# A hybrid encoder layer: the HGRN2 mixer in blocks of 704 tokens with seven block products

## The reference

```python
q, f, i, g = split(rmsnorm(x) @ w_in)               # 1024 -> 4 x 1024, 8 heads of 128
fg = lb + (1 - lb) * sigmoid(f); k = 1 - fg; G = cumsum(log(fg))     # in chunks of 64 tokens
scores = tril((q * exp(G - g_mid)) @ (k * exp(g_mid - G)).T)
o = scores @ i + (q * exp(G)) @ state
state = exp(g_last) * state + (k * exp(g_last - G)).T @ i
x = x + (rmsnorm(o) * silu(g)) @ w_out
x = x + (silu(h @ w_gate) * (h @ w_up)) @ w_down     # h = rmsnorm(x), 1024 -> 2816 -> 1024
```

## Time and profile before

| | |
|---|---|
| time, median of 3 runs | 2577.03 us (2571.08 to 2577.51) |
| the profiled execution | 2580.97 us, its span 2579.2 us |
| instructions | 42643, of them 14834 matmuls |
| TensorE busy | 2495.8 us, 97% of the span |
| VectorE, ScalarE, GpSimd busy | 70%, 53%, 22% |
| mean granted TensorE clock | 0.993 of full |
| DMA | 508.59 MB, 197 GB/s over the span |

### The profile page before, as it was taken

The page is one execution under the profiler, slowest core; times in us unless marked ns, Lnnn a source line. Parts: engine busy times, 40 slices in busy tenths (PEclk is TensorE's granted clock), DMA queues, the critical chain, the costliest instruction groups (busy, mean ns, idle before and its releaser), DMA issues.

```text
span 2579.2 us, 42643 instructions
## 1 busy us (share of the span) xinstructions
PE 2495.8 (97%) x14834; PEld 2341.2 (91%) x14834; DVE 1798.6 (70%) x2620; ACT 1355.0 (53%) x2370; POOL 576.0 (22%) x411
## 2 busy tenths in 40 slices
PE   7999999999999999998999999999999999999899
PEld 7999888887888778887999999999999999899899
DVE  6666556775776566767667767677666778878777
ACT  5555535655655555644455445555444545555454
POOL 6333233343554243420211012011101100000000
PEclk9999999999999999998999999999999999999999
DMA  7433565446556576535666656665657677877875
GB/s 266 157 117 116 161 202 174 141 139 229 176 188 202 160 243 192 195 105 169 204 203 194 211 185 207 203 199 185 195 177 242 209 245 235 273 252 233 291 227 186
DMA packets 263102, 508.59 MB, mean 197 GB/s; under 512 B 28432, under 2 KB 100144, under 8 KB 252608
## 3 DMA queue, kind: packets, MB, share of 16 engines
q1 hardware_dynamic: 262560, 498.10, 60.3%
q0 software_dynamic: 384, 8.44, 0.9%
HBM read 396.11 MB, written 116.65 MB: 199 GB/s over the span
## 4 chain that ended last, share of the span: by engine, by line
PE 75%; DMA 7%; DVE 7%; issue 5%; ACT 3%; SPq 2%; POOL 1%; DVEq 0%; ACTq 0%; POOLq 0%
PE ps L517 9%; PE ps L519 9%; PE ps L518 9%; PE ps L611 8%; PE ps L613 8%; PE ps L612 8%; DMA w_raw<-sum_d 4%; PE ps_o L611 2%; PE ps_o L613 2%; PE ps_o L612 2%; PE ps_k L611 2%; PE ps_k L613 2%; PE ps_k L612 2%; DMA w_raw<-raw_d 1%; DVE w_lo L1157 1%
## 5 line engine op out<-in xcount | busy, mean ns | idle before, releaser
L833 ACT ACTIVATE w_hi<-w_raw 128x512 fp32r<-128x512 f32 (+1 forms) x711 | 438.8, 618 | 638.0 <-PE ps L613 289.4
L1157 DVE TENSOR_TENSOR w_lo<-w_raw,w_hi 128x512 fp32r<-128x512 f32 (+1 forms) x711 | 508.5, 718 | 366.8 <-ACT w_hi L833 364.3
L611 PE MATMUL ps<-rows,w_hi 128*128 128x352 f32 x1584 | 518.6, 327 | 21.3 <-DVE rows L1148 14.4
L612 PE MATMUL ps<-rows,w_hi 128*128 128x352 f32 x1584 | 511.9, 323 | 0.0
L613 PE MATMUL ps<-rows,w_lo 128*128 128x352 f32 x1584 | 511.7, 323 | 0.0
L517 PE MATMUL ps<-h_hi,w_hi 128*128 128x512 f32 (+1 forms) x1280 | 470.5, 368 | 16.9 <-DVE h_lo L947 10.0
L519 PE MATMUL ps<-h_hi,w_lo 128*128 128x512 f32 (+1 forms) x1280 | 452.4, 353 | 0.0
L518 PE MATMUL ps<-h_lo,w_hi 128*128 128x512 f32 (+1 forms) x1280 | 452.3, 353 | 0.0
L942 DVE TENSOR_TENSOR w_lo<-w_raw,w_hi 128x512 fp32r<-128x512 f32 x320 | 266.8, 840 | 203.8 <-ACT w_hi L794 202.7
L611 PEld LDWEIGHTS ps<-rows,w_hi 128*128 128x128 f32 x1584 | 299.3, 189 | 27.5 <-DVE rows L1148 16.6
L612 PEld LDWEIGHTS ps<-rows,w_hi 128*128 128x128 f32 x1584 | 301.8, 191 | 0.2
(11 more groups left out here) (204 smaller groups left out, 4791.3 us busy)
## 6 DMA issues: line engine op xcount, KB each, us to landing
w_raw<-w_all SPq DMA_DIRECT2D x518, 256.0 KB, 3.3
w_raw<-sum_d SPq DMA_DIRECT2D x408, 256.0 KB, 3.7
act_d<-za SPq DMA_DIRECT2D x33, 1232.0 KB, 6.2
quads<-w_all SPq DMA_DIRECT2D x272, 128.0 KB, 2.8
sum_d<-quads SPq DMA_DIRECT2D x34, 1024.0 KB, 4.5
w_raw<-raw_d SPq DMA_DIRECT2D x108, 256.0 KB, 4.4
hx<-x_d SPq DMA_DIRECT2D x96, 176.0 KB, 3.7
zp<-act_d SPq DMA_DIRECT2D x19, 704.0 KB, 6.5
```

The lines of the kernel that those rows point to most:

```text
L611: pe.matmul(bank, w_hi[:, ring, k, :], moving[:, 0, turn, :], start=begin, stop=False, skip_group_check=True)
L612: pe.matmul(bank, w_hi[:, ring, k, :], moving[:, 1, turn, :], start=False, stop=False, skip_group_check=True)
L833: nc.scalar.activation(w_hi[:, r, 0:kn, :], w_raw[:, r, 0:kn, :], ACT.Copy).then_inc(w_hi_ready, 1)
L1157: nc.vector.tensor_tensor(w_lo[:, r, 0:kn, :], w_raw[:, r, 0:kn, :], w_hi[:, r, 0:kn, :].bitcast(F32), ALU.subtract).then_inc(w_lo_ready, 1)
```

## The change

The mixer gets the FFN's scheme. It takes the 2112 tokens in three blocks of 704, with the prompt first and the 64 tokens of the running stream at the end of the third block (`runs` cuts a load or store where the layout in memory needs it). The input projection of a head is two groups of seven products (f and g, then v and q), 48 groups in all; the output projection is four groups a block, 12 in all, behind all heads. The reciprocal root of the norm is now applied to `x` ahead of the product, in `scale_tile`; a block's four rows are made by the code that made the FFN's. Rows 0 and 1 of the next block are made in the last two heads of a block, rows 2 and 3 at the start of the block, in whose first group `mix_group` goes by rows and not by products.

A head's finished output is stored to DRAM (`y_d`) and comes back as a row for the output projection; the residual `x` is loaded again for it (`xo`). The recurrence of head H - 1 has six units (five pairs of chunks and one chunk) in eight steps behind pieces 1 to 8 of the fourteen of head H. Heads are no longer a loop; every instruction is written out.

20 more sums of quadrants are needed (16 for the input, 4 for the output projection), 54 in all: two with a tile of their own before the first product, two more before the first head, then two a head and three in heads 12 and 18. Sums 42 to 53, those with a raw store, come in heads 18 to 23. In the FFN, results and residuals of the down projection go by ScalarE's queue, but for the last two groups.

The core of the diff (TensorE, VectorE, ScalarE, GpSimd, SP, in this order):

```diff
-            def head(b, T, h, recur):
...
+            def turn_values(R):
+                pe.wait_ge(m_cd_read, 2 * R + 2)
+                pe.wait_ge(m_a_read, 2 * R + 2)
+                wait(pe, ssum_ready, unit(R, 0))
+                wait(pe, y32_ready, R)
+                for p in range(4):
+                    mm = pe.transpose(ps_u[:, p * P:(p + 1) * P], v_row[:, p * P:(p + 1) * P], ident[:])
...
+            def mix_group(gm, H, by_rows):
...
+                    for k in range(HK):
+                        row_needed(gm, k, 2)
+                        for p in range(4):
+                            if k == 0:
+                                pe.wait_ge(w_lo_ready, PROD * gm + p + 1)
+                            one(gm, p, k, k == HK - 1)
+                        if 0 < H and k < 3:
+                            for u in ((0,), (1,), (2, 3))[k]:
+                                recurrence(H - 1, u)
...
+            for gm in range(MIX + OUTS):
+                H = gm // 2
+                mix_group(gm, H, gm in (0, 2 * HEADS, 4 * HEADS, MIX))
...
+            def block_begin(H):
...
+                row_low(base + 1, 1)
+                if H > 0:
+                    recurrence(H - 1, 0)
+                block_row(blk, 2)
+                row_low(base + 2, 0)
+                row_low(base + 2, 1)
+                if H > 0:
+                    recurrence(H - 1, 1)
+                block_row(blk, 3)
+                if H > 0:
+                    recurrence(H - 1, 2)
+                row_low(base + 3, 0)
+                row_low(base + 3, 1)
...
+            def recurring(H, s):
+
+                if s == 0 and H > 0:
+                    scaled_queries(H - 1)
+                if begins_block(H) and s == 0:
+                    if H > 1:
+                        finish_output(H - 2)
+                    block_begin(H)
+                elif s == 1 and H > 1 and not begins_block(H):
+                    finish_output(H - 2)
...
+            def head(H):
+                for s in range(SPAN):
+                    if s in (6, 13):
+                        mix_results(2 * H + s // PROD)
+                    split_lo(SPAN * H + s + LEAD)
+                    if s in (5, 12):
+                        mix_middle(2 * H + s // PROD)
+                    recurring(H, s)
...
+                if s == 0 and H > 0:
+                    first_values(H - 1)
+                    if H > 1:
+                        out_rstd(H - 2)
...
+            def store_result(g, n):
...
+                for done, col, size in runs(t, HC):
+                    act.dma_start(y_view[m, :, col:col + size], tile[:, done:done + size]).then_inc(y_stored[i], 16)
...
+                mix_ends(2 * H)
...
+                for n in sums[:-1]:
+                    quad_sums(n, quads)
+                if squared:
+                    add_square(0, blk + 1, 2 * h)
+                gates(H)
+                mix_ends(2 * H + 1)
+                keys(H)
+                if squared:
+                    add_square(1, blk + 1, 2 * h + 1)
+                quad_sums(sums[-1], quads)
...
+            def sum_events(H, s):
+                ns = sums_of_head(H) if H < LAST else []
+                before = EARLY_SUMS - 1 if H == 0 else sums_of_head(H - 1)[-1]
+                if s == 1:
+                    store_sums(before)
...
+                if s == 2:
+                    load_quads(ns[0])
+                if s == 4:
+                    store_raws(ns[0])
+                if len(ns) == 2:
+                    if s == 7:
+                        store_sums(ns[0])
+                    if s == 9:
+                        load_quads(ns[1])
+                    if s == 11:
+                        store_raws(ns[1])
...
+            first_quads(0)
+            first_quads(1)
...
+            load_quads(2)
+            store_sums(0)
+            for n in range(FIRST_PIECE):
+                load_mix_piece(n)
...
+                if n >= PROD:
+                    events(n - PROD)
```

More of the change, by code:

```diff
@@ L305, in wait @@
[L305 to L327 removed]
+        return row[:, UNIT * p + P:UNIT * (p + 1)]
@@ new lines, in base_of, with loads_of, hx_count, xo_count @@
+    def base_of(blk):
+        return HK * blk
+    def loads_of(nb):
+        return len(runs(TF * nb, TF)) if nb < FBLOCKS else 1
+    def hx_count(slot, nb, turn):
+        done = sum((HK + HK) * loads_of(n) for n in range(1, nb))
+        here = turn // 2 if turn < KT else HK + turn - KT
+        return 16 * (done + (here + 1) * loads_of(nb))
+    def xo_count(n):
+        return 16 * sum(2 * loads_of(i // HK) for i in range(n + 1) if i % 2 == n % 2)
+    def quad_loads(n):
+        return 8 if n >= SUM_DN else 4
@@ L329, in product_step, with quads_count, result_stores, y_count @@
+    def quads_count(n):
+        return 16 * sum(quad_loads(i) for i in range(2, n + 1))
+    def result_stores(blk):
+        return 2 * (len(runs(TF * blk, HC)) + len(runs(TF * blk + HC, HC)))
+    def y_count(blk):
+        return 16 * sum(result_stores(b) for b in range(blk))
     def product_step(g):
@@ new lines, in one @@
+            def one(gm, p, k, end):
+                n = PROD * gm + p
+                row = HK * (gm // (2 * HEADS)) + k if gm < MIX else rows_of(gm - MIX - OUTS)[k]
+                bank = (mix_cd[:, 0, :], mix_cd[:, 1, :], mix_b, mix_a)[(0, 1, 2, 3, 0, 1, 3)[p]]
+                turn, ring, moving = (0, 2, 1, 3, 6, 5, 4)[p], n % RING, rows[place_of(row)]
+                pe.matmul(bank, w_hi[:, ring, k, :], moving[:, 0, turn, :], start=k == 0 and p < 4, stop=False, skip_group_check=True)
+                pe.matmul(bank, w_hi[:, ring, k, :], moving[:, 1, turn, :], start=False, stop=False, skip_group_check=True)
+                mm = pe.matmul(bank, w_lo[:, ring, k, :], moving[:, 0, turn, :], start=False, stop=end, skip_group_check=True)
+                if end:
+                    mm.then_inc(pieces_done, 1)
@@ L1359, in _ @@
             dve.wait_ge(bound_ready, 1)
-            for b in range(BLOCKS):
-                block_program(b, T0 if b == 0 else TB)
+            for u in range(LEAD):
+                split_lo(u)
+            for H in range(LAST):
+                head(H)
+            for i in range(OUTS):
+                out_group(i)
             for g in range(GROUPS):
@@ new lines, in load_head_row, with store_head @@
+            def load_head_row(row):
+                blk, k = divmod(row - ROW_OUT, HK)
+                sp.wait_ge(row_lo_ready, 2 * row)
+                for half in range(2):
+                    H = HEADS * blk + HK * half + k
+                    sp.wait_ge(heads_stored, 16 * (H + 1))
+                    target = zp[:, 3:PROD + 1:4, :] if half == 0 else zp[:, 4:PROD:2, :]
+                    sp.dma_start(target, halves(y_d.ap()[H])).then_inc(y_row_loaded, 16)
+            def store_head(H):
+                sp.wait_ge(y32_ready, H + 1)
+                sp.dma_start(y_d.ap()[H], osq[:]).then_inc(heads_stored, 16)
```

2022 lines of the change are left out of this document (1034 added, 988 removed).

## The result

Four runs of the changed kernel have a median of 2875.68 us (2872.39 to 2883.52), the kernel before beside them 2577.27; the ratio is 1.115 (1.113 to 1.117). The forecast was 2644 in a range up to 2695: the direction held, the size and, as the last sections show, the reason did not. The profiled execution took 2878.67 us, its span is 2876.9.

A forecast was written before the change was run, and what follows sets the result against it. The mixer was taken as bound by the columns TensorE streams. Terms -109 + 6 - 33 + 39 + 49 + 21 + 12 + 9 + 70 + 18 - 15 = +67 gave a median of 2644 us, range 2535 to 2695.

The forecast's parts named there:

- The start: Before the first heads: sums, stores, loads and four rows delay TensorE, a loss of 58 us against 19: +39 (30 to 45).
- Block changes: Heads 8, 16 and first output group wait for rows: +49 (30 to 60); row-making in heads 6, 7, 14, 15: +12.
- The FFN: Results of the last stretch go by ScalarE's queue, no longer ahead of pieces on SP's: -15 us (-35 to 0).
- the raw sums: Heads 18 to 23: twelve quadrant sums with raw stores on one tile outlast TensorE's work: +70 us (36 to 80).
- A head's chain: Each head's end: TensorE waits for VectorE's output of the head before, 1.5 us in 14 heads: +21 (0 to 35).
- VectorE and GpSimd take turns: Rival, chance 0.13: in the heads GpSimd's work stretches VectorE's instructions; 39 to 40 us a head, 2693 (2670 to 2730).
- The clock is not charged: Whole kernel: no time added for TensorE's clock, which was 0.96 in the start and 1.00 in the heads.
- The recurrence was taken at 9.0 us: Each of 24 heads: TensorE's recurrence takes 9.0 us (8.6 to 9.4), 216 in all against 210 before: +6.
- head 12: Three sums of weight quadrants in this head take 46 us: +9.
- Output groups: Output projection: VectorE needs 15 us a group against TensorE's 13.4, and loads come late: +18 (0 to 30).
- products and old waits: Mixer: projection matmuls fall from 916 to 806 us, -109; waits at block changes and in heads go, -33.

The follow-up runs named there:

- the ten runs: The ten profiled runs whose FFN is that of the changed kernel; in them the FFN took 1370.0 to 1378.5 us.
- the additions shortened: Changed kernel with the four additions of each sum of weight quadrants on 8 columns instead of 512; 2729.33 us.
- one run: Changed kernel with rows 4 to 11 of the heads' outputs not loaded back from DRAM in the output projection; 2866.40 us.
- the later recurrence: Changed kernel with the recurrence of the head before starting behind piece 3 instead of piece 1; alone 2818.55 us.
- another order on VectorE: Changed kernel with the later recurrence, plus `chunk_ends` and `double_steps` moved to the end of step 13, `scaled_queries` to step 2; 2836.96 us.

## Why the prediction was wrong

**What held.** All 5040 products are there, 0.160 apart. The start: first product on `rows` at 41.1 (forecast 35 to 40), and 45 of them by 69.9, a loss of 63 us where 58 was forecast. Block changes: heads 6 to 8, 14 to 16 and 23 lost 71 us over ordinary heads, forecast 49 + 12 (by its own terms 45 + 12: 24 less 12.2 is 11.8, not 14). The FFN: -27.5 (-19 by the longest of the ten runs), inside -35 to 0. That heads from 18 on wait for sums held too. That the sign held is luck in part: the forecast was slower because of the raw sums, +70 in a sum of +67, and of these some 20 showed; most of the loss came from a term that it had at 21.

**The step that failed is "A head's chain", forecast 1.5 us a head and +21.** Ordinary heads of the first two blocks exceed 39 us by far (46.7 in heads 1 to 4, 47.2 in heads 9 to 11), which the forecast itself named as a sign of being wrong. The chain was worked out with VectorE's durations free of GpSimd. All 24 heads together took 1205.0 us (from the first head's snapshot to the first of the output projection); 24 times TensorE's own 36.8 is 883, block changes 71, the excess of heads 18 to 22 over ordinary ones 20. What is left is 231, 9.6 a head. In heads 9 to 11 (10.4 each) the runs divide it: 6.8 goes with the additions, 6.1 of it with the last sum; with these gone, 1.7 is the wait for the output, close to the forecast's 1.5, and 1.8 that for the sums of block products, which the forecast had at nothing. So the order of the chain was right, and the lengths in it were not. The rival "VectorE and GpSimd take turns" had this mechanism, and even the right busy time of VectorE, 33 a head, and was priced at 39 to 40 a head and 2693 us. It laid the stretching evenly over the head, against VectorE's spare time. But the second sum of each head ran beside the 12 us of VectorE's work at the head's end that TensorE waits for. GpSimd's order, in which the last sum stands behind `keys`, laid in time beside VectorE's chain would have shown it.

The Trainium skill's "SBUF — State Buffer", section "SBUF: two separate sides", has this as an exclusive lock for a whole instruction with two inputs in SBUF, or in VectorE's two-port mode. The trace agrees: 1.77 for 0.68, and 0.88 with an input in PSUM beside GpSimd or not.

**"The clock is not charged" failed with it.** Behind the waits of 6 us products ran at the lower level: 0.93 in the heads, 0.80 at a block change, 2.4 us of the 6.8 a head. With the additions shortened the heads were back at 1.00.

**The recurrence was taken at 9.0 us, with bounds 8.6 and 9.4.** TensorE's busy time of a head at the full clock is 36.8, less 26.9 for its products: 9.9, and +28 over 24 heads, not +6.

**Sums, forecast +70 and +9 for head 12.** A chain of 46 us a head is right for heads from 18 on in kind: SP waits 62 us of 155 in it. But it is laid beside heads of 47, so that only some 20 of it show; head 12, with three sums, took 46.7, no more than its neighbours.

**Output groups, forecast +18.** Eleven periods took 222 us against 148 of products. The last head's recurrence, 9.9, is in them and also in the 24 times 36.8 above, so that some 10 of these 74 belong to the heads. VectorE was counted by its work, 15 a group, as if it could do it in any order; it stood behind rows that wait for ScalarE, for loads and once for a store; that reading rests on the waits of the trace and on one run. Groups 8 to 10, whose rows come from the residual and not from the heads, took 17 to 18, nearer to the count.

These terms are the 325 of the mixer, to 1 us: 44 for the start, 28, 71, 231, 20 and 74, and -109 and -33 as forecast for products and old waits. As the 231 is a remainder, that the sum closes proves nothing; what the runs show of it is the division in heads 9 to 11.

**What stays open.** How the output projection's loss divides, and how much of the start could be had by another order. No variant of the changed kernel came near the kernel before: with additions next to nothing and the later recurrence it still took 2687.

## What to carry to other kernels

That a helper engine is idle does not make its work free: before adding some, lay it in time beside the chain that the bound engine waits for, instruction by instruction, and count a stretched chain, not a busy share. When work is moved to make room for such a chain, ask what is queued behind its result; here one queue held both the results of the sums and the weights. And a wait of some us on TensorE should be charged twice, once for itself and once for the clock behind it.

## What the runs showed that was not expected

The stretching works both ways, and on one-input copies. VectorE's scan, with two inputs in SBUF, kept its 1.62 us; GpSimd's addition that came 0.04 us after it took 2.33, where 0.94 is enough (557.33). Rows of VectorE, then of GpSimd, in the changed kernel:

```profile
581.71 1.62 DVE L1110 TENSOR_TENSOR_SCAN sums_c<-scan_keep,decay 128x704 f32<-128x704 f32 x1
```

```profile
557.33 0.94 POOL L1555 TENSOR_TENSOR s<-s 128x352 f32<-128x352 f32 x1 [6.28 <-ACT s L732]
...
581.75 2.33 POOL L1555 TENSOR_TENSOR s<-s 128x352 f32<-128x352 f32 x1 [1.75 <-ACT s L732]
```

The copy of 11 columns (L1129 above), a single input, took 1.54 us beside GpSimd's keys and began 0.19 us after them; it ended as they did. In the run with another order on VectorE, where GpSimd is idle at that place, all 24 of these copies took 0.16 to 0.17.
